# Attention output in seven products of halves, gate logits in column groups, a later far step and another order of experts, in a two-block fp32 model kernel

## The reference, cut to what matters

```python
# first block, layer 0: latent attention; layer 1: neighbourhood attention
y  = o.reshape(B, S, H * DV) @ w_o           # 16 heads of 64 -> 1024, all 512 tokens
x  = layer_norm(ALPHA * x + gate * y)         # gate from ada_w, ada_b, one per segment
...
return (silu(g) * a) @ w_out                  # conv_ffn, hidden 2816
# second block
gates  = sigmoid(h @ w_gate)                  # 24 columns of w_in: 8 heads x 3
o_hg   = rmsnorm(o_hg) * silu(g)              # recurrence's output
for e in range(32):                           # hier_moe, 2 experts chosen per token
    hid = silu(t @ w_gate[e]) * (t @ w_up[e])
    out = out + combine[:, e:e+1] * (hid @ w_down[e])
```

## Time and profile before

| | us |
|---|---|
| median of 3 runs | 1923.35 (1923.25 to 1924.73) |
| the profiled execution | 1930.62 |
| its span in the trace | 1928.9 |
| busy PE / DVE / ACT | 1761.5 / 893.9 / 362.7 |
| experts, from the first gate product | 1484.20 to the end |

### The profile page before, as it was taken

One profiled execution on the slowest core, in us unless ns is written; L12 is line 12 of the kernel. 1 busy time (PEld: TensorE's weight loads), 2 busy tenths in 40 slices (PEclk: granted clock), 3 DMA queues, 4 the chain that ended last, 5 costly groups with the idle time before them and its releaser, 6 DMA issues.

```text
span 1928.9 us, 33169 instructions
## 1 busy us (share of the span) xinstructions
PE 1761.5 (91%) x14152; PEld 1363.9 (71%) x14152; DVE 893.9 (46%) x1909; ACT 362.7 (19%) x859; POOL 0.2 (0%) x4
## 2 busy tenths in 40 slices
PE   7999999999999999999999999999999766666666
PEld 4455546888888887777888888888788554555545
DVE  1488837766667327667554412478333211111112
ACT  0343403111110014222211102202321100000001
POOL 0000000000000000000000000000000000000000
PEclk9999999999999999999999999999999987888889
DMA  9534321222221207445344543323286999999996
GB/s 377 223 132 165 142 87 44 88 87 87 87 103 65 116 33 229 153 154 196 120 146 159 206 165 131 131 74 124 88 351 252 421 429 429 428 428 428 429 428 267
DMA packets 32508, 395.64 MB, mean 205 GB/s; under 512 B 3616, under 2 KB 6688, under 8 KB 8736
## 3 DMA queue, kind: packets, MB, share of 16 engines
q1 hardware_dynamic: 32416, 394.31, 51.2%
HBM read 393.25 MB, written 1.05 MB: 204 GB/s over the span
## 4 chain that ended last, share of the span: by engine, by line
PE 77%; DMA 19%; DVE 2%; ACT 1%; issue 1%; SPq 0%; DVEq 0%
PE bank L547 23%; DMA ring<-w_moe 17%; PE bank L1759 13%; PE bank L600 8%; PE bank L1487 6%; PE bank L3211 3%; PE bank L1972 3%; PE bank L843 2%; PE bank L1968 1%; PE bank L753 1%; PE bank L1145 1%; DMA ring<-w_ada 1%; PE bank L2328 1%; PE bank L1121 1%; PE bank L2024 1%
## 5 line engine op out<-in xcount | busy, mean ns | idle before, releaser
L547 PE MATMUL bank<-layer_input,ring 128*128 128x256 f32 x1152 | 257.4, 384 | 0.0
L547 PEld LDWEIGHTS bank<-layer_input,ring 128*128 128x128 f32 x1152 | 220.5, 193 | 33.1 <-issue 3.0
L3211 PE MATMUL bank<-ring,arena 128*32 128x128 f32 x1920 | 77.3, 326 | 54.6 <-DMA ring<-w_moe 52.1
L3328 DVE TENSOR_TENSOR arena<-arena,bank 128x128 f32<-128x128 f32 x32 | 9.2, 288 | 230.6 <-PE bank L3211 230.6
L1759 PE MATMUL bank<-arena 128*128 128x256 f32 x504 | 115.6, 379 | 0.0
L3211 PEld LDWEIGHTS bank<-ring,arena 128*32 128x32 f32 x1920 | 66.3, 131 | 66.5 <-DMA ring<-w_moe 61.8
L1487 PE MATMUL bank<-arena,ring 128*128 128x256 f32 x480 | 107.0, 380 | 2.4 <-ACT arena L1582 1.4
L1759 PEld LDWEIGHTS bank<-arena 128*128 128x128 f32 x504 | 95.8, 190 | 13.0
L1487 PEld LDWEIGHTS bank<-arena,ring 128*128 128x128 f32 x480 | 90.7, 190 | 16.5 <-ACT arena L1582 2.8
L600 PE MATMUL bank<-arena,ring 128*128 128x256 f32 x452 | 99.1, 380 | 0.9 <-DVE arena L2131 0.6
L3211 PE MATMUL bank<-arena 128*32 128x128 f32 x2008 | 70.2, 297 | 28.9 <-DMA arena<-w_moe 27.6
(11 more groups left out here) (484 smaller groups left out, 2708.7 us busy)
## 6 DMA issues: line engine op xcount, KB each, us to landing
arena<-w_moe SPq DMA_DIRECT2D x46, 2048.0 KB, 26.5
ring<-w_moe SPq DMA_DIRECT2D x45, 2048.0 KB, 25.9
ring<-w_ffn_in SPq DMA_DIRECT2D x22, 2048.0 KB, 8.0
ring<-w_ada_late SPq DMA_DIRECT2D x8, 3072.0 KB, 10.0
ring<-w_ffn_out SPq DMA_DIRECT2D x8, 2816.0 KB, 9.6
ring<-w_proj SPq DMA_DIRECT2D x7, 3072.0 KB, 10.2
ring<-w_na_pair SPq DMA_DIRECT2D x8, 1536.0 KB, 6.3
arena<-w_far SPq DMA_DIRECT2D x11, 1024.0 KB, 6.9
```

The source lines that it names most:

```text
L547: last = pe.matmul(out, a, b, start=(k == 0), stop=(k == len(lhs) - 1))
L3211: ins = eng.matmul(bank[x][group[q], 0:P], xe[:, k, SLOTS * e:SLOTS * e + SLOTS], weight(e, last, (x * KT + k) * FE + q * P, P), start=(k ...
```

## The change

All of it is in one diff, with these parts.

1. `out_split` becomes `split_out`, with a dictionary of what differs, and `mla_out` calls it: eight tiles of heads are halved into two times four (`HALF_HEADS`), so product i is four calls of 256 columns. There are 28 products and no rest. The order is written by `split_steps`. w_mla_o is cut into four chunks of 2048 columns. `phase_end` behind the heads is gone; the first product waits for the copy of head pair 3, the second (1,1) follows it, and (0,2) waits for that of pair 7. The opening's semaphores are used again for it.
2. The last pair's chunk of `ada_late` has five tiles and one mid row, not four and two. In every pair the first mid row stands in `maxima`, ahead of its second wait. The last pair has eight fill calls ahead of `turn` and a different order on DVE.
3. Step 6 of both uses of the seven products: `rest` is a step of its own, `FAR_REST`, between 6 and 7.
4. The gate logits are 8 calls with 32 stationary columns in four column groups, 256 tokens wide (`gate_sums`), a DVE copy of 256 columns behind the memset, and two calls with a new constant `fold24` behind the spread; the fill behind them is 3 calls, not 4.
5. ACT makes the recurrence's squares and copies at turn 4.
6. The kept expert is number 2. Quad 0 is straight code; slots go by (e + 1) % 2. Expert 3 is loaded where 0 was, 4 where 1 was, and from 5 on each where the second before it was, third by third. The first, empty scatter is gone, with the memsets of `gwt` and `y`. In the last quad 28 and 29 are scattered behind the gate of 30, the gate of 31 is multiplied behind the up of 30, experts 30 and 31 are scattered alone, each with 32 rows, and the last quarter of down of 31 has a semaphore of its own.

The core of the diff:

```diff
-HALF_K = 10
-OUT_ORDER = [(0, 1), (0, 2), (1, 1), (1, 2)] + [(c, n) for c in (0, 1) for n in (3, 4, 5, 6, 7)] + \
-    [(c, n) for c in (2, 3) for n in range(1, 8)]
...
+HALF_K, HALF_HEADS = 10, 4
+FAR_REST = 8
+def split_steps(done_0, snapped_0, rest):
+    late = (6, FAR_REST, 7) if rest else (6, 7)
+    first = ((0, 1), (0, 2), (1, 1), (1, 2)) if rest else ((0, 1), (1, 1), (0, 2), (1, 2))
+    order = list(first) + [(c, n) for c in (0, 1) for n in (3, 4, 5) + late] + \
+        [(c, n) for c in (2, 3) for n in (1, 2, 3, 4, 5) + late]
...
@@ mla_heads
-        self.phase_end(eng, who)
@@ mla_heads_pe
             ada(u, 0)
+            if u == ADA_LAST:
+                b = claim(("av", u))
+                self.fill(pe, 8, b)
             turn(u)
@@ mla_heads_dve, maxima
+            mid(u, 0, 0)
             dve.wait_ge(s["scored"], 2 * u + 2)
@@ mla_heads_dve, the loop
-            mid(u, 0, 0)
             turned(u)
-            mid(u, 0, 1)
...
+            if u < ADA_LAST:
...
+            else:
+                ada(u)
+                mid(u, 0, 1)
+                attended(u)
@@ mla_out
-        self.layer_step(who, eng, "mla_o", lambda k: self.A[:, k, :], KT, 4, 2, 0, (0, 1), lambda k: squares[:, k, :],
-                        1, 0, 3, 4)
+        self.split_out(who, eng, s, dict(
+            name="mla_o", source=self.A[:, :, :], half=HALF_HEADS, nk=KT, steps=HEAD_STEPS, sums=OPENED["vector_in"],
...
@@ split_out, step
                 if i == 6:
...
-                    eng.wait_ge(s["up_used"], used_0 + c)
-                    rest(d, c, 1, CTX, start=True)
-                    last = product(a, w21, t3, False)
+                    last = product(a, w21, t3, False)
+                if i == FAR_REST:
+                    eng.wait_ge(s["up_used"], used_0 + c)
+                    last = rest(d, c, 1, CTX, start=True)
@@ the mixer, PE
+        def gate_sums():
+            w = VOFF["w_gate24"][0]
+            for k in range(KT):
+                j = 32 * (k % 4)
+                last = pe.matmul(bank[6][j:j + 32, 0:LAT], self.V[:, w + k * 24:w + k * 24 + 32], x[k], start=(k < 4),
+                                 stop=(k >= 4), skip_group_check=True)
...
         def gate_logits():
+            pe.wait_ge(s["cmp_steps"], self.GATE_COPIED)
             for t in range(2):
-                last = self.mm(pe, bank[6][:, t * 24:(t + 1) * 24], [xk[:, t * P:(t + 1) * P] for xk in x],
-                               [self.vec("w_gate24", k * 24, 24) for k in range(KT)])
+                last = pe.matmul(bank[6][:, LAT + t * 24:LAT + (t + 1) * 24], sums[:, t * P:(t + 1) * P],
+                                 self.con("fold24"), start=True, stop=True)
...
         first_groups()
+        gate_sums()
+        spread()
         gate_logits()
-        spread()
-        self.fill(pe, 4)
+        self.fill(pe, 3)
@@ the mixer, ACT
-            if u == 5:
+            if u == 4:
@@ the experts
-RESIDENT = EXPERTS - QUAD
+RESIDENT = 2
...
+        for x in (RESIDENT + 1, RESIDENT + 2):
+            for part, used in enumerate(parts_used):
+                sp.wait_ge(used, x - RESIDENT)
+                self.load_part(sp, x, x - RESIDENT - 1, part)
+        with sp.Fori(0, (LAST - RESIDENT - 3) // 2) as it:
             for e in range(2):
                 for part, used in enumerate(parts_used):
-                    sp.wait_ge(used, it * 2 + e + 1)
-                    self.load_part(sp, it * 2 + e + 2, e, part)
+                    sp.wait_ge(used, it * 2 + e + RESIDENT + 2)
+                    self.load_part(sp, it * 2 + e + RESIDENT + 3, e, part)
...
+        def scatter_alone(e, turn):
+            for t in range(2):
+                for h in ((turn + t) % 2, (turn + t) % 2 + 2):
+                    q = group[(h + e) % 4]
+                    ins = eng.matmul(bank[4 + 2 * t + h // 2][:, (h % 2) * 256:(h % 2) * 256 + 256], gwt[q, h, t, :],
+                                     alone[e][q, :], start=False, stop=(e == QUAD - 1), skip_group_check=True)
...
+                    if last and e == 2:
+                        eng.wait_ge(s["silu_done"], x + 1)
+                        project(0, QUAD - 1, last=True).then_inc(s["gate_done"], 1)
```

More of the change, by code:

```diff
@@ L1445, in ffn_split, with split_out @@
         {"pe": self.ffn_split_pe, "dve": self.ffn_split_dve, "act": self.ffn_split_act}[who](eng, s, v)
-        self.out_split(who, eng, s, v)
-    def out_split(self, who, eng, s, v):
-        g, b = [self.vec(f"ln2_{x}", 0, KT) for x in "gb"]
-        ga, ba = self.next_gains(who, eng, g, b, 1, 0, 1)
+        hid = [2 * HALF_K, FT]
+        self.split_out(who, eng, s, dict(
+            name="ffn_out0", source=v["hid"], half=HALF_K, nk=FT, steps=OUT_STEPS, sums=3 * (FT - 1) + 4, used=FT,
+            gate=5, ln=2, to=(1, 0, 1), spare=[self.ring[i][:, 5632:6144] for i in range(2)], squares=[self.A[:, k, :] for k in range(KT)],
+            arrived=lambda part: eng.wait_ge(s["hid_done"], hid[part])))
+    def split_out(self, who, eng, s, o):
+        g, b = [self.vec(f"ln{o['ln']}_{x}", 0, KT) for x in "gb"]
+        ga, ba = self.next_gains(who, eng, g, b, *o["to"])
+        order, done, snaps, snapped = o["steps"]
+        half, nk, squares = o["half"], o["nk"], o["squares"]
         self.a_base = self.claim(who, a_ready=KT)["a_ready"]
@@ L1492, in rest @@
                 slot = self.ring[(g0 + c) % 2]
-                for k in range(2 * HALF_K, FT):
-                    o = (x * FT + k) * P
-                    last = eng.matmul(out, slot[:, o:o + P], hid[:, k, col:col + 256], start=(start and k == 2 * HALF_K),
-                                      stop=(k == FT - 1), skip_group_check=True)
+                for k in range(2 * half, nk):
+                    o = (x * nk + k) * P
+                    last = eng.matmul(out, slot[:, o:o + P], src[:, k, col:col + 256], start=(start and k == 2 * half),
+                                      stop=(k == nk - 1), skip_group_check=True)
                 return last
@@ L1560, in spread @@
                 last.then_inc(n["rstd_spread"], 1)
-            for c, i in OUT_ORDER:
+            for c, i in order:
                 step(c, i)
@@ L3198, in one_hots, with place, weight @@
             ins.then_inc(s["g_ready"], 1)
-        def weight(e, last, at, n):
-            if last and e == 0:
+        def place(e, first):
+            return (0, 1, None, 0)[e] if first else (e + 1) % 2
+        def weight(e, first, last, at, n):
+            if first and e == RESIDENT:
                 return self.kept_weight(at, n)
@@ L3204, in weight, with project @@
                 return self.held_weight(at, n)
-            return slots[(e - last) % 2][:, at:at + n]
-        def project(x, e, last):
+            return slots[place(e, first)][:, at:at + n]
+        def project(x, e, first=False, last=False):
             for k in range(KT):
@@ L3272, in quad @@
                     eng.wait_ge(down_in, arrived)
-                    down(e, last)
+                    down(e, first, last)
                     if e < 2:
@@ L3284, in moe @@
                 .then_inc(rs["var_ready"], 1)
-            with eng.Fori(0, quads - 1) as i:
+            quad(0, first=True)
+            with eng.Fori(1, quads - 1) as i:
                 quad(i)
-            quad(quads - 1, True)
+            quad(quads - 1, last=True)
             eng.wait_ge(s["y_dve"], EXPERTS + 1)
-            eng.wait_ge(s["y_act"], EXPERTS + 1)
-            for t in range(2):
-                scatter(t, stop=True).then_inc(self.sem("var_ready"), 1)
+            eng.wait_ge(link, quads + 8)
+            scatter_alone(3, 0)
+            eng.wait_ge(link, quads + 12)
+            scatter_alone(3, 1)
         def copy_rows(x, e, copy, groups, sem):
@@ L3313, in quad @@
                         copy_xe(i + 2)
-                    copy_rows(x, e, eng.copy, (2, 3), "y_act")
+                    if last and e == 2:
+                        eng.wait_ge(s["down_done"], x + 1)
+                        eng.copy(alone[e][64:128, :], bank[2][64:128, 0:256]).then_inc(s["y_act"], 1)
+                    elif not last or e < 2:
+                        copy_rows(x, e, eng.copy, (2, 3), "y_act")
             eng.nop().then_inc(s["y_act"], 1)
@@ L3346, in quad @@
                         copy_xe(i + 2)
-                    copy_rows(x, e, eng.tensor_copy, (0, 1), "y_dve")
+                    if last and e == 2:
+                        eng.wait_ge(s["down_done"], x + 1)
+                        eng.tensor_copy(alone[e][0:64, :], bank[2][0:64, 0:256]).then_inc(s["y_dve"], 1)
+                    elif last and e == QUAD - 1:
+                        eng.wait_ge(s["down_done"], x + 1)
+                        eng.tensor_copy(alone[e], bank[2][:, 0:256]).then_inc(s["y_dve"], 1)
+                    else:
+                        copy_rows(x, e, eng.tensor_copy, (0, 1), "y_dve")
+                    if last and e == 0:
+                        for n in range(2, QUAD):
```

(2 more changed lines are left out.)

253 lines of the change are left out of this document (153 added, 100 removed).

## The result

| us | before | after |
|---|---|---|
| median | 1923.82 (4 runs, 1923.25 to 1924.73) | 1913.33 (4 runs, 1910.44 to 1916.13) |
| the profiled execution | 1930.62 | 1916.13 |
| its span | 1928.9 | 1914.3 |
| ratio, 95% interval | | 0.9945 (0.9928 to 0.9962) |

Faster by 10.5 us of the medians (the interval: 7 to 14), where 14.3 was forecast. 1913.33 lies inside the range of 1903 to 1915, above the forecast's own 1906.5 to 1911.5. The two profiled executions differ by 14.5, nearly the forecast.

What follows compares the result with a forecast made beforehand. PE was taken to bound the kernel until about 1487 us, then the experts' weight stream by DMA. Gains 2.4+2.1+1.6+5.0+3.2 = 14.3 gave 1909.0 for the median, range 1903 to 1915.

Steps and rivals of the forecast that it cites:

- The carried difference: Closing step: gain summed against the profiled run, 1930.62, 7.3 above the median of 1923.35, then taken off the median.
- Recurrence: Recurrence's sum: earlier ACT copies remove a 1.59 wait and the half-speed clock behind it; gain 5.0.
- the rival of 1.6: Recurrence's sum: idle time goes, but another wait replaces it and half speed stays; 1.6 for 5.0; chance 0.08.
- Attention output: Heads' end and output stage: 6.9 less PE work from shorter products, partly eaten by waits; gain 2.4.
- Chunk 1: Attention output's second weight chunk lands late, at 245.8; PE idles 3.1, with 1.9 of half clock charged again.
- Far rows: Feed-forward, steps 6 and 7: two far-row calls fill the 0.64 snapshot wait; gain 2.1.
- Gate logits: Mixer's front: 16 instructions on four column groups replace 32, next projection starts earlier; gain 1.6, ends 0 and 3.8.
- the clock stays up: Rival: full speed behind chunk 1 and in the gates' stretch, no tail gap; 5.1 more, 1904; chance 0.16.
- Experts: Experts' tail: down(31) 2.3 earlier, first sum another 0.9, half an issue gap charged; gain 3.2.
- Exposed snapshots: Rival at attention output: short products expose 28 snapshots of 0.64, leaving gain 0.2, no change; chance 0.06.
- A dry stream: Slower rival: expert weight stream runs dry at its head, near 1520, since later loads wait for expert 3; chance 0.04.
- Edits at nothing: Priced at zero: mid row in the maxima's wait, fifth ada tile ahead of turn(7), dropped memsets and first scatter.

Runs made afterwards that it cites:

- b1: The kernel before, unedited, once more in the profiler: span 1922.2 us.
- a1: The changed kernel run again without an edit: 1911.58 us (6 runs), ratio 0.9946 to the kernel before.
- a2: The changed kernel with the recurrence's squares and copies back at turn 5: 1914.14 us, ratio 0.9954 to the kernel before.
- b3: The changed kernel with the old gate logits (32 instructions of 24 columns, fill 4, no copy): 1916.27 us, ratio 0.9958 to the kernel before.
- c1: The changed kernel with the far rows' two calls ahead of product 6 again: 1917.02 us, ratio 0.9956 to the kernel before.
- c2: The changed kernel with DVE's copy of the gate sums ahead of the memset, which moves behind the fourth eviction: 1911.37 us, ratio 0.9929.
- b4: The changed kernel without the eight fill calls ahead of turn(7): 1912.03 us, ratio 0.9934 to the kernel before.
- a3: The changed kernel with the old attention output (512-column calls, two 2 MB loads, phase meeting), heads' order kept: 1910.39 us, ratio 0.9930.
- a4: The changed kernel with the old experts' part (28 kept; loads, scatters and memsets undone): 1914.80 us, ratio 0.9953 to the kernel before.
- c3: The changed kernel with the second half of expert 30's scatter behind the last down product: 1912.74 us, ratio 0.9945 to the kernel before.

## Why the prediction was right or wrong

The direction, the range (1903 to 1915) and the size within a third held; 1909.0 was 4.3 too low. The sum of the parts came out for the execution on which it was made, and was wrong to carry over to the median whole. That 14.3 met the 14.6 between the first two profiles is partly luck: the output gave more than I had, the experts less, and the opening took 1.8.

- **The carried difference.** The step that failed is "its gain is taken off the median". The profile's span stood 6.7 above the typical one (1922.2), which I noted and didn't ask about. b1 shows where: half speed behind the recurrence's wait (3.3), more of it in the mixer's front (1.8), the experts' stretch (1.6). A gain worked out from a stretch that the median doesn't have isn't in the median. From b1's span to the mean of "after" and a1 (1911.8) it is 10.4, the medians' 10.5.
- **Recurrence, 5.0 forecast.** 5.0 between the first profiles, 1.7 by a2 and by b1 against a1. I gave 0.08 to the rival of 1.6 and called it "the clock falls anyway"; it is that the clock as a rule didn't fall. Size wrong: 3.3.
- **Attention output, 2.4 forecast for heads and stage.** Measured 1.4 and 3.1 ("after"), where the clock stayed up; with it down (a2, b3, c1, c2: stages of 69.0 to 69.6) 1.4 and 0.9 to 1.5, nearly the 1.3 that I had for the stage. Chunk 1 was late as said, somewhat less: counted from the heads' end its product ran at 4.2 where I had 4.8, idle 2.27 where I had 3.1. The heads' gain I had from the fill and from DVE's copies; it is the clock over the transposes (b4). And the stage's gain isn't the seven products' (a3: 0.4), it is the shorter idle time at the phase's end and the clock. The "6.9 less" of PE work was sized rightly call by call, but PE's busy time fell by 4.2 only and its idle time rose from 1.5 to 5.3 (a3 and a1). The load rule that the prediction quotes from the Trainium skill ("DMA: Bandwidth & Descriptors", Anatomy of one DMA) is fitted there to loads that GpSimd issues. SP issues them here, and the four chunks of 1 MB took 4.9 in the median from issue to landing, against 4.4 by the rule.
- **Far rows, 2.1.** 2.2 by c1's rows. The step is right.
- **Gate logits, 1.6, ends 0 and 3.8.** Between the first two profiles the front gave 1.0 (1206.57 to 1213.79 is 7.22, 1201.37 to 1207.56 is 6.19), 0.6 short of the forecast; the copy waits for the memset, as I had it. But the clock was at half in part of both. With it up the front takes 5.12 (a1), 0.5 less than the 5.63 that I had. Against the old products the part is worth 0.9 at the same clock and 4.2 where the clock falls with them only (b3 against a1), 4 to 5 in time: at the upper end of what I gave, and the part of the rival "the clock stays up".
- **Experts, 3.2.** 2.5 by stretches, 3.2 by a4's time. Down(31) came 2.5 earlier in its stretch (474.41 to 471.92) where I said 2.3, but b1 and a4 have 472.85 and 472.89 with the old order, and the nine profiles 471.6 in the mean: 1.3. The last scatter gave 1.2 where I took 0.9. No issue gap was left in the last quad, the order of PE's own work cost its place instead (c3). In quad 0, which is straight code now, "after" has two such gaps, 0.54 and 1.97, so straight code doesn't keep them away.
- **Other rivals.** Exposed snapshots: three of 0.46 and not 28. A dry stream: none. Edits at nothing: the mid row in the maxima's wait left the heads' pairs as they were, 17.51 and 21.46 in turn (17.55 and 21.46 before; they aren't all some 17.5 long, as the description of the kernel has it).

The errors were of both signs. From b1 to the mean of "after" and a1: 3.3 too much at the recurrence, 0.8 at the experts, 0.6 at the far rows and gates together, 1.2 lost in the opening, and 2.1 too little at heads and output; together 3.8, the distance from 14.3 to 10.5.

## What to carry to other kernels

Before a profile's terms are summed, compare its span with the median: if it lies above, find the stretches at half clock, and count a gain there only once a second profile of the same kernel shows them again. When PE work is cut by short products, list what each of them waits for: here 6.9 us of matmuls became 0.4, and reordering one product to cover a load gave more (2.0) than the whole change of method. To compare small edits, cut the traces at the same points, and learn how well each stretch repeats: with the change the heads took 148.71 to 148.73 in twelve profiles and the recurrence 190.89 to 190.96 in eleven, but the stretch to down(31) 470.5 to 473.2 in nine, where the whole varies by 9.

## What the runs showed of the hardware that I had not expected

- The same wait of 1.59 us had a granted clock of 0.50 behind it in one execution and 1.00 in two others (b1, a2). Ahead of the second chunk it stayed up behind idle times of 1.73 (b4), 1.97 (a4), 2.11 (a1), 2.27 ("after") and 2.77 (c3), and fell behind 2.18 (b3), 2.35 (a2), 2.43 (c1) and 2.83 (c2), so the length of the wait doesn't decide it. Elsewhere it stayed up behind 1.16 (a3) and 1.97 (b4) and fell behind 1.86 (a4, a wait for the feed-forward's output weights: a window of 0.60).
- In the mixer's front of the kernel before and of b3 it fell with no idle time of PE ahead: 0.55 in a window in which PE was busy 4.00 of 4.00 us (b3).
- The opening's first 20 matmuls of 512 columns took 8.85 to 11.05 us (c3) in different executions while the windows of the two first profiles give a granted clock of 1.00 and DMA at over 400 GB/s there. I don't know why.
- Products with 32 rows a call, on different groups of rows: eight instructions of 256 columns in 0.71, where sixteen with 128 rows took 3.72. That is 0.09 each against 0.23; by the forecast's reckoning, two groups side by side, it would be 0.12.
